# First block's feed-forwards: two gate-and-up tiles computed whole instead of three, twenty by seven products

## The reference, cut to what matters

```python
h = _rmsnorm(x, norm_ffn[layer])
gu = h @ ffn_w_gu[layer]
x = x + (jax.nn.silu(gu[..., :FFN_HIDDEN]) * gu[..., FFN_HIDDEN:]) @ ffn_w_down[layer]
...
jnp.split(jax.nn.silu(c) @ ada_w[i] + ada_b[i], 6, axis=-1)
```

## Time and profile before

| | us |
|---|---|
| median of 3 runs | 2819.39 (2818.64 to 2819.72) |
| the profiled execution | 2819.84 |
| span in its trace | 2818.0 |
| PE busy | 2744.8 (97% of the span) |
| DVE, POOL, ACT busy | 1136.6, 536.2, 519.8 |
| first feed-forward, gate and up: first half unit to last quad | 411 to 704 |
| second feed-forward, the same | 1133 to 1406 |

### The profile page before, as it was taken

The page is one execution under the profiler, slowest core; times in us unless marked ns, Lnnn a source line. Parts: engine busy times, 40 slices in busy tenths (PEclk is TensorE's granted clock), DMA queues, the critical chain, the costliest instruction groups (busy, mean ns, idle before and its releaser), DMA issues. The chain is left out here.

```text
span 2818.0 us, 36275 instructions
## 1 busy us (share of the span) xinstructions
PE 2744.8 (97%) x15260; PEld 1785.2 (63%) x15260; DVE 1136.6 (40%) x2212; ACT 519.8 (18%) x1154; POOL 536.2 (19%) x371
## 2 busy tenths in 40 slices
PE   8999999999999999999999999999989999998998
PEld 5444477777886445888887745788833337873333
DVE  2325533444412233444442274666232235643223
ACT  1424420000001232111000231434011011011011
POOL 1000003233341010244442210011010004431000
PEclk9999999999999999999999999999999999999999
DMA  8211025775222221222121400210289982229994
GB/s 265 94 42 55 30 90 217 270 271 194 83 97 86 90 82 36 89 90 90 64 86 49 169 16 16 85 33 10 120 345 420 421 338 75 90 104 366 421 421 200
DMA packets 70042, 431.13 MB, mean 153 GB/s; under 512 B 8202, under 2 KB 9017, under 8 KB 25720
## 3 DMA queue, kind: packets, MB, share of 16 engines
q1 hardware_dynamic: 65080, 412.48, 38.2%
q0 software_dynamic: 4800, 16.33, 1.7%
HBM read 422.33 MB, written 13.79 MB: 155 GB/s over the span
## 5 line engine op out<-in xcount | busy, mean ns | idle before, releaser
L467 PE MATMUL bank<-h,weight_ring 128*128 128x256 f32 x912 | 218.8, 383 | 1.1 <-DVE arena L391 1.0
L467 PEld LDWEIGHTS bank<-h,weight_ring 128*128 128x128 f32 x912 | 170.6, 190 | 36.9 <-issue 13.3
L1287 PE MATMUL bank<-h,weight_ring 128*128 128x512 f32 (+2 forms) x464 | 179.7, 539 | 0.6 <-DVE h L273 0.6
L3387 PE MATMUL bank<-h,weight_slots 128*128 128x256 f32 (+1 forms) x576 | 173.3, 455 | 0.8 <-ACT h L2529 0.8
L622 PE MATMUL bank<-arena,weight_ring 128*128 128x256 f32 x704 | 155.0, 379 | 0.0
L3387 PEld LDWEIGHTS bank<-h,weight_slots 128*128 128x128 f32 x576 | 107.3, 190 | 64.7 <-issue 47.2
L622 PEld LDWEIGHTS bank<-arena,weight_ring 128*128 128x128 f32 x704 | 133.7, 190 | 18.6 <-issue 0.4
L2862 PE MATMUL bank<-weight_slots,tokens_T 128*64 128x512 f32 x592 | 141.6, 593 | 2.1 <-issue 2.1
L467 PE MATMUL bank<-h,arena 128*128 128x256 f32 x608 | 143.6, 379 | 0.0
L1287 PEld LDWEIGHTS bank<-h,weight_ring 128*128 128x128 f32 (+1 forms) x464 | 84.8, 188 | 89.4 <-issue 86.0
L467 PEld LDWEIGHTS bank<-h,arena 128*128 128x128 f32 x608 | 115.5, 190 | 15.7
(11 more groups left out here) (552 smaller groups left out, 4517.6 us busy)
## 6 DMA issues: line engine op xcount, KB each, us to landing
arena<-in_ada_w SPq DMA_DIRECT2D x48, 1024.0 KB, 5.0
weight_ring<-in_gu SPq DMA_DIRECT2D x44, 1024.0 KB, 5.0
weight_slots<-in_w_up SPq DMA_DIRECT2D x42, 1024.0 KB, 26.2
weight_slots<-in_w_down SPq DMA_DIRECT2D x34, 1024.0 KB, 21.9
weight_slots<-in_w_gate SPq DMA_DIRECT2D x32, 1024.0 KB, 23.3
weight_ring<-in_w_gate SPq DMA_DIRECT2D x32, 1024.0 KB, 23.3
weight_ring<-in_w_down SPq DMA_DIRECT2D x30, 1024.0 KB, 23.8
weight_ring<-in_down SPq DMA_DIRECT2D x32, 704.0 KB, 4.1
```

The lines of the kernel that those rows point to most:

```text
L467: m = pe.matmul(self.bank(q, i), weights[:, c * P:(c + 1) * P], tokens[:, c, :], start=(c == 0), stop=(c == 3))
L1287: m = pe.matmul(out, lhs, rhs, start=(c == 0), stop=(c == last - 1))
L3387: m = pe.matmul(self.bank(n)[:, 0:hi - lo], slot.buf[:, at:at + P], self.h[:, c, lo:hi], start=(c == 0), stop=(c == KT - 1))
```

## The change

`HEAD` goes from 3 to 2 for both feed-forwards: two whole tiles (four half units) and twenty quads. What follows from it is moved along: the parts of the modulation inside the quads start two earlier (`ada_between`), since two half units are gone, and the last steps of the modulation stand in quad 17 instead of 16; DVE makes the first two token differences behind the same multiply; pair differences and the copying out of part groups are called one quad later by number. The order in which SP issues its loads is not edited.

```diff
 class GatedUnits:
-    HEAD = 3
+    HEAD = 2
...
                 def ada_between(q, i):
-                    n = 4 + 3 * q + i
+                    n = 2 + 3 * q + i
                     if n < mod.parts:
                         mod.part(pe, n)
-                    elif q == 16 and i == 0:
+                    elif q == 17 and i == 0:
                         mod.turn(pe)
...
                     for n in range(1, len(gate.units)):
                         gate.multiply(v, n)
-                        if n <= 4:
-                            gate.differ(v, n - 1)
+                        for i in {1: (0, 1), 2: (2,), 3: (3,)}[n]:
+                            gate.differ(v, i)
                     gate.pair_differ(v, 0)
                     group(-1)
                     for q in range(gate.quads):
                         gate.quad_multiply(v, q)
-                        if q % 2 == 0:
+                        if q % 2 == 1:
                             gate.pair_differ(v, q // 2 + 1)
                         group(q)

                 def ada_rows(q):
                     for g in range(mod.GROUPS):
-                        if (mod.PARTS * (g + 1) - 5) // 3 == q or g == 0 and q < 0:
+                        if (mod.PARTS * (g + 1) - 3) // 3 == q:
                             mod.keep(v, g)
-                    if q == 16:
+                    if q == 17:
                         mod.add(v)
```

## The result

| | before | changed |
|---|---|---|
| median of 18 runs each, side by side | 2819.89 us (2818.39 to 2825.75) | 2824.91 us (2820.65 to 2830.81) |
| ratio, 95% interval | | 1.0017 (1.0011 to 1.0024) |
| profiled execution, span | 2819.84, 2818.0 | 2824.45, 2822.7 |

The changed kernel is 0.17% slower, some 5.0 us. That is clear of noise, but inside the 0.2% (5.6 us) that the prediction called no change and inside its range (2818.0 to 2829.0), 3.3 us above its 2821.6. The profiled executions are 4.6 us apart.

A forecast was written before the change was run, and what follows sets the result against it. PE, busy 2744.8 of 2818.0 us, was taken as the bound. From 2819.84, less 3.45 for the trade, plus 4.1 for the first wait and 1.6 for margins, gave 2822.1, as a median 2821.6 us; range 2818.0 to 2829.0.

The forecast's parts named there:

- What one tile costs: Both feed-forwards: a whole tile takes PE 13.81 us, a tile by seven products 12.09; 1.73 us won each, 3.45 together.
- The start of the stage, one tile earlier: Third half unit and first products by seven, both feed-forwards: tokens and token differences still arrive in time; cost nothing.
- The first new wait: First feed-forward, part 5: panel 5 queues behind tile 7's later load, so PE stands 4.1 us (bounds 4.0 and 5.4).
- Thirteen thin margins: Later tiles of the first feed-forward: panel 3k lands 0.5 us before its part; two late cases charged, 1.6 us (0 to 3.5).
- The rule on bandwidth: Paired loads: at 358 GB/s the second lands at 7.9 us, first wait 4.5, sum 0.4 us more; not adopted.
- Every pair is late: Rival 1, first feed-forward: second loads land after 8.6 us, PE waits 0.65 us in thirteen tiles; 2829.6 us, chance 0.20.
- The clock: Rival 2, behind the wait at part 5: idle PE loses its clock, 1.7 us more, 2823.3 us; chance 0.18.
- The sum: Whole program: 2819.84 - 3.45 + 4.1 + 1.6 = 2822.1, as a median 2821.6 us; called no change, forecast chance 0.50.

The follow-up runs named there:

- the kernel with all tiles moved: Changed kernel with the loads of tiles 7 to 20 issued one panel later; 2817.01 us against 2820.64 for the kernel before, ratio 0.9986.
- the six profiles: Profiles of six kernels, the changed one included, with later tile loads still paired with panels; 0.6, 0.3, 2.3, 0.0, 1.2, 0.0 us lost at the margins.
- the experiment by filling: Changed kernel, loads of tiles 8 to 20 one panel later, none, four or nine dummy matmuls before part 5: 2821.84, 2823.36, 2821.33 us; kernel before 2820.84.

## Why the prediction was right

**What one tile costs**: right. 1.73 us in the second feed-forward, and 1.73 in the first once nothing waits.

**The start of the stage, one tile earlier**: right in both feed-forwards. The third half unit and the first quad wait for nothing new. DVE's and POOL's added 12 us each are hidden, as the full stage of the kernel with all tiles moved shows.

**The first new wait**: right in place, cause and size. 3.96 us measured, 4.1 predicted; part 5, behind tile 7's load; and moving that load alone undoes it.

**Thirteen thin margins**: right in kind, high in size. The charge was 1.6 us, two cases of 0.8; the changed kernel's profile has two cases of 0.37 and 0.22, and the six profiles lost 0.7 on average, 0 to 2.3.

**The rule on bandwidth**: by the 358 GB/s of the Trainium skill, DMA: Bandwidth & Descriptors, Where 436 GB/s comes from, the estimate was that the panel of each pair lands 7.9 us after the tile's issue. It landed at 7.5 in the median, 7.3 to 8.3 in fourteen pairs; the core moved 418 GB/s while part 5 waited, and eleven of thirteen margins held. The rows were the better source for the median, but their single pair hid the spread that costs the margins.

**Every pair is late**: did not happen. The first rival's 8.6 us belongs to loads that follow each other by 1.9 us; at 0.4 the second landed in the median 7.5 after the first was issued.

**The clock**: this is what the forecast left out. The second rival came true on top of the forecast, with a chance of 0.18 where it should have had most: it happened in all five profiled executions that had the 4.0 us of idleness. It cost 2.6 us in that of the changed kernel, just above the upper of its two bounds (1.7 and 2.5), and 1.6 to 3.0 over the five.

**The sum**: the forecast stood 2.25 us above the kernel before, the measured time 5.0 above it, 2.8 more; the other 0.5 of the 3.3 us is the kernel before itself, whose median was 2819.39 in three runs and 2819.89 in eighteen. With 2.6 for the clock, which the sum had at nothing, and 0.6 for the margins instead of 1.6 it would be 2819.89 - 3.45 + 3.96 + 2.6 + 0.6 = 2823.6. The remaining 1.3 us is within what separates two comparisons of the same two kernels (+5.0 and +2.8). There is some luck in the answer "no change": one term was 1.0 us too high and one 2.6 too low, and +5.0 lies close under the 5.6 us from which it would have been called slower.

**Small slips in the working**: the earlier trace rows give 0.75 as the busy share of the DMA engines in the first feed-forward, not 0.77. The first rival's threshold leaves out the trade and the first wait; with them it passes 5.6 us from a landing of 8.3 on, not 8.4. Neither moves the forecast.

What stays open is how much of the clock's price reaches the median. The changed kernel's executions had a mean granted clock of 0.9971 and 0.9978 in the two comparisons (the kernel before 0.9981 to 0.9983); 0.001 of the clock is 2.8 us of the span, so this says 1.3 to 2.9 us, an estimate. The medians of the experiment by filling did not confirm it.

## What to carry to other kernels

A change that swaps one tile for another also swaps what the tile's buffer waits for. Where one queue issues loads for two consumers strictly in order, look for each load whose condition moved and for the loads behind it: here one load, which kept the panel behind it waiting for 7 us after that panel's own condition was met (part 3 ended at 451.5, the panel went out at 458.5), turned a gain of 3.45 us into a loss of 5.0, and moving it behind one other load left a gain of 2.8. When a wait of 4 us on PE appears, price the half clock behind it as well, here 1.6 to 3.0 us. Where medians cannot resolve a term, compare the length of its stage in the profiles.

## What the runs showed of the hardware

With 4.0 us without work PE's granted clock fell to 0.50 in all five profiled executions: in three of them while PE still waited, in two as the work began again. In the changed kernel's it stayed there for the first 5.4 us of the work behind. With 2.2 to 2.3 us without work it fell in one of two executions, and with no idle time it fell in none of four.

Such slow stretches also appear where PE is busy, at a few places of the program and at each in only some of the executions: at 1765.7 us in the kernel before, at 24 us in the profiled execution of the changed one, and neither has the other's. The stretch of the changed one:

```profile
24.00:27.20 3.20, 3.20 (x8) 2.54 (x8) 3.20 (x10) 0.00 (x0) 0.40 (x1) 0.50 0.01 3
```

They go with the spread of the times: over the 93 executions of the kernel before in the three series, those with a mean granted clock of 0.999 took 2819.6 us on average, those with 0.998 took 2820.8 and those with 0.997 took 2823.3. So 11 executions resolve no less than some 2 us here.

Of two loads of 1 MB that go out 0.4 us apart, the first lands some 4.9 us and the second 7.5 us (7.3 to 8.3) after the first issue. In the pairs 1.9 us apart the second lands 8.6 us after it in the median, later than the one that was issued sooner; there the panel goes first and the tile second, and no run separates the order from the distance.
